# First condition by halves of the channels, weights and condition in separate slots: one change to a fused two-block kernel on one core

## What is computed

```python
c_act = silu(c)
cond = c_act @ ada_w + ada_b                     # 1024 x 6144 weights, one row
shift1, scale1, gate1, shift2, scale2, gate2 = split(cond, 6)
h = rmsnorm(x, norm1_g) * (1 + scale1) + shift1
u, v, val, gate = split(h @ w_in + b_in, 4)      # 512 columns each
y_a = rmsnorm(gelu(u) * mixed(layernorm(gelu(v))))
y_b = rmsnorm(silu(layernorm(conv31(val * sigmoid(gate)))))
x = x + gate1 * (concat(y_a, y_b) @ w_out)
# then a feed-forward with shift2, scale2, gate2 of 2816 columns, a final norm with its own condition
# then the second block: projections, sparse attention, cross attention, and 32 experts of three 1 MB matrices each
```

## Time and profile before

| what | value |
|---|---|
| three runs | 792.23, 792.97, 793.47 us; median 792.97 us |
| the profiled execution | 789.66 us, of it 787.9 us span of the core |
| PE busy | 719.9 us (91%), 5423 matmuls |
| DVE busy | 366.7 us (47%) |
| ACT busy | 326.4 us (41%) |
| bytes loaded | 209.5 MB, 267 GB/s over the span |

### The profile page before, as it was taken

One profiled execution on the slowest core, in us unless ns is written; L12 is line 12 of the kernel. 1 busy time (PEld: TensorE's weight loads), 2 busy tenths in 40 slices (PEclk: granted clock), 3 DMA queues, 4 the chain that ended last, 5 costly groups with the idle time before them and its releaser, 6 DMA issues.

```text
span 787.9 us, 13085 instructions
## 1 busy us (share of the span) xinstructions
PE 719.9 (91%) x5423; PEld 563.0 (71%) x5424; DVE 366.7 (47%) x745; ACT 326.4 (41%) x696; POOL 60.8 (8%) x71
## 2 busy tenths in 40 slices
PE   6798999889999999999999999997999998778785
PEld 4385678787999999999988777785865554344352
DVE  1452998554755444555478679544441111011011
ACT  2243485363743333454448896668421111001001
POOL 5000002000000000100000009062000000000000
PEclk9899899889999999999999999999999999899899
DMA  8997856633966656553554436355999999999994
GB/s 317 406 372 286 304 219 268 237 107 109 370 215 215 214 179 215 202 182 135 178 187 148 157 108 222 107 214 213 343 393 422 419 422 420 422 420 421 418 406 142
DMA packets 71476, 211.44 MB, mean 268 GB/s; under 512 B 7352, under 2 KB 34134, under 8 KB 55543
## 3 DMA queue, kind: packets, MB, share of 16 engines
q1 hardware_dynamic: 70370, 209.91, 70.3%
q0 software_dynamic: 800, 0.63, 0.5%
q10 hardware_dynamic: 244, 0.03, 0.0%
HBM read 209.51 MB, written 1.05 MB: 267 GB/s over the span
## 4 chain that ended last, share of the span: by engine, by line
PE 67%; DMA 15%; DVE 7%; ACT 6%; issue 3%; SPq 2%; ACTq 0%; DVEq 0%
PE ps L1906 10%; PE ps L1907 9%; PE ps L1908 9%; DMA ring<-in_expert_w_gate_dram 7%; PE ps L1919 5%; PE ps L2590 5%; PE ps L1920 5%; PE ps L1921 5%; DMA ring<-in_expert_w_up_dram 4%; PE ps L1988 3%; DMA ring<-in_ada_w_dram 2%; SPq L431 2%; DVE ring_low L1177 2%; PE ps L2632 2%; PE ps L2561 2%
## 5 line engine op out<-in xcount | busy, mean ns | idle before, releaser
L1177 DVE TENSOR_TENSOR ring_low<-ring,HI 128x1024 fp32r<-128x1024 f32 (+1 forms) x119 | 142.3, 1237 | 45.9 <-ACT HI L667 45.8
L667 ACT ACTIVATE HI<-ring 128x1024 fp32r<-128x1024 f32 (+1 forms) x135 | 133.9, 1056 | 42.4 <-DMA ring<-in_w_in_dram 41.4
L1906 PE MATMUL ps<-AH,HI 128*128 128x256 f32 x320 | 90.1, 282 | 0.3 <-DVE Z L1423 0.3
L1908 PE MATMUL ps<-AH,ring_low 128*128 128x256 f32 x320 | 89.6, 280 | 0.0
L1907 PE MATMUL ps<-AL,HI 128*128 128x256 f32 x320 | 89.5, 280 | 0.0
L2590 PE MATMUL ps<-ring,ZM 128*32 128x256 f32 x880 | 73.6, 422 | 16.1 <-DMA ring<-in_expert_w_up_dram 11.2
L1906 PE MATMUL ps<-HI,AH 128*128 128x512 f32 (+1 forms) x176 | 71.6, 407 | 2.1 <-DVE ring_low L1177 1.0
L1907 PE MATMUL ps<-ring_low,AH 128*128 128x512 f32 (+1 forms) x176 | 68.9, 392 | 0.0
L1908 PE MATMUL ps<-HI,AL 128*128 128x512 f32 (+1 forms) x176 | 68.5, 389 | 0.0
L2590 PEld LDWEIGHTS ps<-ring,ZM 128*32 128x32 f32 x880 | 35.1, 121 | 44.0 <-DMA ring<-in_expert_w_up_dram 14.1
L1906 PEld LDWEIGHTS ps<-AH,HI 128*128 128x128 f32 x320 | 60.1, 188 | 3.1 <-issue 2.5
(11 more groups left out here) (381 smaller groups left out, 1325.8 us busy)
## 6 DMA issues: line engine op xcount, KB each, us to landing
ring<-in_expert_w_up_dram SPq DMA_DIRECT2D x28, 1024.0 KB, 26.3
ring<-in_expert_w_gate_dram SPq DMA_DIRECT2D x27, 1024.0 KB, 26.4
ring<-in_ada_w_dram SPq DMA_DIRECT2D x24, 1024.0 KB, 8.6
ring<-in_expert_w_down_dram SPq DMA_DIRECT2D x23, 1024.0 KB, 23.8
ring<-in_w_ffn_in_dram SPq DMA_DIRECT2D x20, 1024.0 KB, 6.1
ring<-in_w_in_dram SPq DMA_DIRECT2D x17, 1024.0 KB, 5.7
ring<-in_w_ffn_out_dram SPq DMA_DIRECT2D x11, 1024.0 KB, 7.1
ring<-in_w_out_dram SPq DMA_DIRECT2D x8, 1024.0 KB, 4.9
```

The costliest lines, as they stand in the source:

```text
L667: act(HI[:, i % UNITS, 0:w], W.view(name)[:, o:o + w], ACT.Copy).then_inc(s_hi, 1)
L1177: tt(W.low(name)[:, o:o + w], W.view(name)[:, o:o + w], HI[:, i % UNITS, 0:w].bitcast(F32), ALU.subtract).then_inc(s_lo, 1)
L1906: mm(dst, lh, rh, start=start, stop=False)
L1908: return mm(dst, ll, rh, start=False, stop=stop)
```

## The change

1. `ada0k` is loaded and multiplied by halves of the channels. A load of 1 MB now holds 256 rows (two per partition) and, of both shift1 and scale1, the 512 columns of one half; it is issued as two transfers of 0.5 MB. PE does `ada_half(h, kp)`, eight matmuls of 32 by 256; four of them complete shift1 and scale1 for half of the channels, and `columns_half`, `lower_half(h)` on DVE and `upper_half(h)` on ACT make AH and AL for four channel tiles at a time.
2. Value and gate are multiplied by halves of the channels too: value units 0 and 1, gate units 0 and 1, then the second halves. The `ada1k` steps that stood between their units move into `between_v`, two after each unit; the `ada2k` steps move into `between_u` (0, 2, 3 and 3 of them). `condition(2, 7)` on DVE goes behind the normalisation of v, and PE's `columns(2, 7)` behind the first unit of u.
3. The eight slots are divided: four for `ada` loads, four for all others, until `out0`; then one ring again. The order of the loads is a new one.
4. v's bias is loaded to a row of `CN` instead of a slot.
5. The sums of squares of x come from two ACT instructions over whole rows (`accum_out`) instead of four squares by channel and PE's 16 products.
6. POOL waits for the first four `ada` steps before it issues its 17 small loads.

```diff
     def place(self, name, until, dmas=1):
-        s = self.order[self.turn % len(self.order)]
-        self.turn += 1
+        if self.lots is None:
+            s = self.order[self.turn % len(self.order)]
+            self.turn += 1
+        else:
+            lot = self.lots[not name.startswith(self.start)]
+            s = lot[0]
+            lot.append(lot.pop(0))
...
+            def ada_half(h, ks):
+                for k in ks:
+                    load(f"ada0{4 * h + k}", (s_ada, 4 * h + k + 1), *(
+                        (lambda v, i=i: v[:, 1024 * i:1024 * i + 1024].rearrange("p (s n) -> p s n", s=2),
+                         A["ada_w"][:, 0:2048].rearrange("(p k) (s n) -> p k s n", p=P, s=2)[:, 2 * k + i, :, 512 * h:512 * h + 512])
+                        for i in range(2)))
...
-            ada(A["ada_w"], 0, range(7), 0)
-            rows128("in_v0", w_in, 1024, 512, 0, 2)
-            ada(A["ada_w"], 0, (7,), 0)
-            rows128("in_v1", w_in, 1024, 512, 2, 4)
-            rows128("in_v2", w_in, 1024, 512, 6, 2)
-            ada(A["ada_w"], 1, (0, 1), 2048)
+            W.apart("ada", 4)
+            ada_half(0, range(4))
+            rows128("in_v0", w_in, 1024, 512, 0, 4)
+            ada_half(1, (0, 1))
+            rows128("in_g0", w_in, 1536, 512, 0, 4)
+            ada_half(1, (2, 3))
             const(wsv, ...)
-            rows128("in_g0", w_in, 1536, 512, 0, 4)
-            ada(A["ada_w"], 1, (2, 3), 2048)
-            rows128("in_g1", w_in, 1536, 512, 4, 4)
-            ada(A["ada_w"], 1, (4, 5), 2048)
-            load("brow_v", (s_un, S.first["in_u0"] + 1), (lambda s: s[0:1, 0:512], A["b_in"][:, 512:1024]))
+            rows128("in_v1", w_in, 1024, 512, 4, 4)
+            rows128("in_g1", w_in, 1536, 512, 4, 4)
+            sp.dma_start(brow_v, A["b_in"][:, 512:1024]).then_inc(*W.other(BROW))
             rows128("in_u0", w_in, 512, 512, 0, 4)
-            ada(A["ada_w"], 1, (6, 7), 2048)
+            ada(A["ada_w"], 1, (0, 1), 2048)
             rows128("in_u1", w_in, 512, 512, 4, 4)
-            ada(A["ada_w"], 2, (0, 1), 4096)
             sp.wait_ge(s_rp, 3)
             (the memory tokens, 1 MB)
+            ada(A["ada_w"], 1, (2, 3), 2048)
             rows128("in_w0", w_in, 0, 512, 0, 4)
-            ada(A["ada_w"], 2, (2, 3), 4096)
+            ada(A["ada_w"], 1, (4,), 2048)
             rows128("in_w1", w_in, 0, 512, 4, 4)
-            ada(A["ada_w"], 2, (4, 5), 4096)
+            ada(A["ada_w"], 1, (5, 6, 7), 2048)
             rows128("kv_v0", w_kv, 512, 512, 0, 4)
-            ada(A["ada_w"], 2, (6, 7), 4096)
+            ada(A["ada_w"], 2, (0, 1, 2, 3), 4096)
             rows128("kv_v1", w_kv, 512, 512, 4, 4)
-            for h in range(4):
+            ada(A["ada_w"], 2, (4, 5), 4096)
+            rows128("out0", w_out, 0, D, 0, 2)
+            ada(A["ada_w"], 2, (6, 7), 4096)
+            W.together([7, 0, 1, 2, 3, 4, 5, 6])
+            for h in range(1, 4):
...
+            po.wait_ge(s_ada, 4)
             const(rowsc[0:4 * TAPS, :], ...)            # POOL, the first of 17
...
+            for t in range(NT):                         # ACT
+                act(SQA[:, t, :], X[:, t, :], ACT.Square, accum_out=RTS[0][:, t:t + 1]).then_inc(s_sqs, 1)
+            def upper_half(h):
+                hi_to((0, 5)[h])
+                ac.wait_ge(s_m, h + 1)
+                for k in range(4 * h, 4 * h + 4):
+                    act(AH[:, k, :], XR[:, k, :], ACT.Identity, scale=..., bias=...).then_inc(s_ah, 1)
+                    if k % 4 == 1:
+                        hi_to(4 * h + 1)
+            upper_half(0)
+            hi_to(3)
+            upper_half(1)
+            hi_to(7)
...
+            def lower_half(h):                          # DVE
+                ve.wait_ge(s_ada, 4 * h + 4)
+                copy(CN[:, 0, 0:256], ps[7][:, 0:256]).then_inc(s_cn, 1)
+                if h:
+                    lo_to(4)
+                (columns and scales of four channel tiles)
+                for k0 in (4 * h, 4 * h + 2):
+                    (HTM of tiles k0, k0 + 1)
+                    if k0 == 0:
+                        lo_to(0)
+                    (AL of tiles k0, k0 + 1)
+                lo_to(4 * h + 1)
+            lower_half(0)
+            lo_to(3)
+            lower_half(1)
+            lo_to(7)
...
+            ve.wait_ge(s_un, S.first["in_u0"] + 1)      # DVE, ahead of E (line 1286)
...
             (DVE: v normalised, line 1312)
+            condition(2, 7)
+            taps(18, 20)
+            columns(2, 7, C2[:, B1:B1 + 16])
             lo_to(iw + 1 + AHEAD)
-            taps(18, 22)
+            taps(20, 22)
...
+            by_channel(("in_v0",), value, "value", (0, 1, 2, 3), between_first)    # PE; ada_half(1, 0), (1, 1) after unit 1
+            by_channel(("in_g0",), gate, "gate", (), between_second)               # ada_half(1, 2), (1, 3) after unit 0
+            columns_half(1)
...
+            by_channel(("in_v1",), value, "value", (), lambda q: None, 2)
+            by_channel(("in_g1",), gate, "gate", (), lambda q: None, 2)
...
             def between_v(i):
-                ada(2, i)
+                for k in ((0, 1), (2, 3), (4, 5), (6, 7))[i]:
+                    ada(1, k)
...
             def between_u(i):
-                ada(2, 4 + i)
+                if i == 0:
+                    columns(2, 7)
+                if i == 1:
+                    te.wait_ge(s_col, 3)
+                for k in ((), (0, 1), (2, 3, 4), (5, 6, 7))[i]:
+                    ada(2, k)
                 diagonals(3 + i)
```

More of the change, by code:

```diff
@@ L103, in split_order @@
 def split_order():
-    out = ["in_v0", "in_v1", "in_v2"] + [f"{w}{h}" for w in ("in_g", "in_u", "in_w", "kv_v") for h in "01"]
+    out = [f"{w}{h}" for h in "01" for w in ("in_v", "in_g")] + [f"{w}{h}" for w in ("in_u", "in_w", "kv_v") for h in "01"]
     out += [f"out{h}" for h in range(4)] + ["fx0", "fy0"]
@@ L735, in _ @@
                     ACT.Copy).then_inc(s_wt, 1)
-            for u in range(4, 8):
-                hi_to(u + AHEAD)
+            hi_to(S.first["in_u0"] + 1)
             ac.wait_ge(s_rc, 1)
@@ L1254, in _ @@
             copy(cw[:, :, 0:TAPS], ps[6][:, 0:4 * TAPS].rearrange("p (j c) -> p c j", c=4)).then_inc(s_rc, 1)
-            for u in range(4, 8):
-                lo_to(u + AHEAD)
-            condition(2, 7)
+            lo_to(S.first["in_u0"] + 1)
             ve.wait_ge(s_set, PAD)
@@ L1990, in ada, with ada_half, columns_half @@
                 ins.then_inc(s_ada, 1)
+            def ada_half(h, kp):
+                name = f"ada0{4 * h + kp}"
+                te.wait_ge(*W.ready(name))
+                for i in range(2):
+                    for j in range(4):
+                        ins = mm(ps[7][32 * j:32 * j + 32, 0:256], cr[:, 2 * kp + i, :],
+                                 W.view(name)[:, 1024 * i + 256 * j:1024 * i + 256 * j + 256],
+                                 start=(kp == 0 and i == 0), stop=(kp == 3 and i == 1))
+                ins.then_inc(s_ada, 1)
+            def columns_half(h):
+                te.wait_ge(s_cn, h + 1)
+                for x in range(2):
+                    ins = tr(ps[7][:, P * x:P * x + P], CN[:, 0, P * x:P * x + P], ident[:, :])
+                ins.then_inc(s_cnp, 1)
             def columns(i, b):
-                te.wait_ge(s_cn, i)
+                te.wait_ge(s_cn, i + 1)
                 for x in range(4):
@@ L2052, in by_channel, with value, gate, between_first @@
                     between(q)
+            def value(ct):
+                return ps[ct][:, 0:256]
+            def gate(ct):
+                return ps[ct][:, 256:512]
             te.wait_ge(s_xc, 4)
-            by_channel(("in_v0", "in_v1", "in_v2"), lambda ct: ps[ct][:, 0:256], "value", (0, 1, 2, 3), lambda q: q and ada(1, q - 1))
+            def between_first(q):
+                if q == 1:
+                    te.wait_ge(s_col, 1)
+                    ada_half(1, 0)
+                    ada_half(1, 1)
+            def between_second(q):
+                if q == 0:
+                    ada_half(1, 2)
+                    ada_half(1, 3)
+            by_channel(("in_v0",), value, "value", (0, 1, 2, 3), between_first)
+            by_channel(("in_g0",), gate, "gate", (), between_second)
+            columns_half(1)
             te.wait_ge(s_r2, 16 * LOADS2)
```

146 lines of the change are left out of this document (69 added, 77 removed).

## The result

The changed kernel takes 771.67 us (median of 3 runs, 769.43 to 774.03) against 792.97: ratio 0.9721, 95% interval 0.9687 to 0.9756, 21.3 us less. Forecast were 781.6 and a range of 774 to 790. The direction was right, and the size was short by 9.9 us. The profiled execution took 774.03 us (span 772.2), against 789.66 before. Here is the timeline of PE after the change, at the places that answer to the earlier trace rows.

A forecast was written before the change was run, and what follows sets the result against it. Before 140 us it took loads, PE, slot waits, then PE and DVE together as bounds in turn. Transposes 15.4 us earlier, less 4 for a clock fall, gave 11.4: 792.97 - 11.4 = 781.6 us, range 774 to 790.

The forecast's parts named there:

- The sum: Added-up times of the first stages: first value matmul 23.9, gate's end 56.4, v's start 57.4 us.
- the 1.34: PE's time for one `ada_half` step of 16 instructions, from the experts' matmuls at 0.084 us each: 1.34 us.
- the bound of 1.0: One `ada_half` step on PE takes 1.0 us if the columns set the pace, 2.0 if weight loads do.
- XR at 26: Before the first value matmul: with the old sums of squares XR, done at 26 us, would be 3 us late.
- the 6.99 us: PE's 16 products for the sums of squares: 6.99 us, most of it taken as waiting between squares.
- rival (b): First eight `ada` loads arrive late as halves, 5.6 us in all at 320 GB/s: 788.5 us, chance 0.18.
- the 2.93 us a load: First loads land 2.93 us apart per 1 MB, against 2.55 by the windows at 412 GB/s.
- I take a fall, and 4 us lost: Behind PE's 2.9 us wait at `columns(2, 7)`: clock falls, 4 us lost, memory's transposes 11.4 earlier, not 15.4.
- it shifts as a whole: What follows the first stages, PE nearly full from 200 us, moves unchanged with the end of those stages.
- the 1.97 us at 140.18: PE's wait behind the memory's transposes, taken to just cover 2.0 us of added `ada` steps in `between_u(3)`.
- the low end of 774: Better than the other cases: 2.55 us a load and `ada_half` at 1.0 give 774 us, chance 0.05.
- Rival (a): No fall of the clock at `columns(2, 7)`, or a shorter wait: 777.6 us, chance 0.25.

The follow-up runs named there:

- after_again: The changed kernel run again with nothing changed: 773.14 us, ratio 0.9777 to the kernel before; its profiled execution took 769.74 us.
- whole_condition: The changed kernel with the first `ada` weights loaded and used in whole steps, in the new load order: 786.8 us, ratio 0.9909 to the kernel before.
- old_squares: The changed kernel with the old sums of squares, by channel with products on PE: 778.63 us, ratio 0.9827 to the kernel before.
- before_filled: The kernel before with six useless matmuls ahead of `columns(2, 7)` and four in the wait at 140 us: 793.88 us, ratio 1.0023.
- longer_wait: The changed kernel with DVE's `condition(2, 7)` moved behind `taps(18, 20)`, lengthening PE's wait: 781.2 us, ratio 0.9852 to the kernel before.
- slots_3_5: The changed kernel with three slots for `ada` loads and five for the others: 788.62 us, ratio 0.9936 to the kernel before.
- the two delays: The changed kernel with two or four useless matmuls ahead of the feed-forward: 777.74 and 780.63 us, ratios 0.9861 and 0.9886 to the kernel before.
- the second series: Both kernels run again with nothing changed: kernel before 794.32 us, ratio 1.0015; changed kernel 773.14 us, ratio 0.9777.
- spatial_behind: The changed kernel with the spatial weights loaded behind in_g1 and transposed behind in_v1's units: 776.58 us, ratio 0.9782 to the kernel before.

## Why the prediction was right in part, and wrong in size

**Up to v, right but for a fall of the clock.** Forecast were the first value matmul at 23.9 (its own terms add up to 24.2), gate's end at 56.4 and v at 57.4. Measured were 22.73, 56.40 and 57.42 in `after_again`, and 23.21, 59.16 and 60.18 in the first profile, with a fall of the clock that I had put at nothing. The sum has about 2 us of pause there (42.7 to 44.8) and no term for the clock; in five of seven profiles it fell. in_v1 was there at 41.15 against 40.1. `ada_half` cost 1.07 us for its 16 instructions, not the 1.34 I took from the earlier trace rows: 16 instructions of 256 columns take what 8 of 512 take (1.07 and 1.06 us in `whole_condition`), so the columns streamed decide here, the bound of 1.0 that I had named. The sums of squares and POOL's loads cost nothing at gate's end, as said. But that XR at 26 would be late by 3 us was wrong, as `old_squares` shows (first value matmul at 25.04, 1.8 to 2.3 later, and none of it left at gate's end). So was the reading that most of the 6.99 us of the earlier trace rows is waiting between squares. The same 32 instructions take 3.94 us in `old_squares`, and 6.96 in `before_filled`, where the granted clock from 14 to 22 us is 0.50: for the most part it is the half rate. The record of the clock before reads 1.00 there, but the `ada` steps on either side take 1.94 and 1.93 us, their length at half rate.

The loads landed about as reckoned: in_v0 at 19.94 (forecast 21.1), in_g0 at 29.73 (29.8), in_v1 at 41.15 (40.1). But rival (b) did happen, in part. `whole_condition` has the same loads in the same order, as single transfers of 1 MB in pieces of 8 KB, and moves more. The windows are those of the first profile after, and then those of `whole_condition`:

```profile
8.00:12.00 4.00, 4.00 (x35) 2.91 (x37) 2.63 (x6) 2.33 (x5) 0.00 (x0) 1.00 1.05 389
12.00:16.00 4.00, 1.98 (x32) 0.68 (x24) 2.36 (x5) 0.00 (x0) 0.00 (x0) 1.00 1.05 387
```

```profile
8.00:12.00 4.00, 4.00 (x30) 2.29 (x28) 2.75 (x5) 1.92 (x5) 0.00 (x0) 1.00 1.02 429
12.00:16.00 4.00, 1.67 (x20) 0.21 (x16) 2.00 (x5) 0.00 (x0) 0.00 (x0) 1.00 0.98 404
```

Its in_v0 is there at 18.64, and its last `ada` load at 34.03, which in `after_again` PE waits for until 36.51. So the halves pay about 2.5 us of loading for what they gain, where the rival had 5.6 at 320 GB/s; the 2.93 us a load in the sum was long enough to cover it. The Trainium skill (DMA: Bandwidth & Descriptors, Rules for kernel authors) asks for at least 1 MiB a transfer for the most bandwidth. These windows agree in direction, but no run here separates the size of the transfer from its pieces of 2 KB.

**From v to the memory's transposes.** 51.5 us were forecast without a fall, and 50.78 measured in both profiles (60.18 to 110.96). The wait at `columns(2, 7)` was forecast at 2.9 us and measured at 2.41 and 0.86. The step that failed is "I take a fall, and 4 us lost". There was no fall behind that wait. The transposes came 16.0 us earlier without a fall that reached them and 13.2 with the one at 45, where I had 11.4. That a fall there was possible was right, as `longer_wait` shows with 4.86 us; its price was 2.8 us there and not 4. The inference from 3.17 and 3.07 in the kernel before to 2.9 was too sure. At this place five profiles with waits of 2.41 to 2.49 and four with 0.82 to 0.94 had no fall behind them; the ones of 2.66 (in `slots_3_5`) and 4.86 had one. So at this place only longer waits than the measured one fell, each in a single profile, and the one of 2.66 in a kernel whose `ada` loads came late. That the length decides is not shown: ahead of value's second half one length did both. The Trainium skill (TensorE: Matmul & The Clock Gate, What's actually happening) states that the chip watches activity by a schedule of its own, which isn't tied to the kernel. The pair of 2.94 and 2.95 there agrees with it. A forecast should have carried a chance for a fall at each of the two waits, instead of a fall taken into the sum at one and nothing at the other.

**Behind it.** The second failed step is that "it shifts as a whole". I had seen the 1.97 us at 140.18 only as cover for the two added `ada` steps, and reckoned nothing for the slow matmuls behind it. In the kernel before it takes 29.65 us from the first to the second squares, in both profiles. After, it takes 28.03 and 26.48: 1.6 to 3.2 us more gained. Behind the wait of 1.97 the clock fell, and the 16 matmuls of one column took 2.85 and 2.87 us, for what took 1.92 after; behind the 0.25 the 16 run at the full rate, as they do in `before_filled` with its wait filled (1.84). The 1.6 us between the two profiles after go with a brief fall from 128 to 134 us in the first. From the second squares to the end the distance is indeed the same: 618.1 and 617.1 before, 617.2 and 617.0 after. That all four of these profiles have it short is luck: eleven of the other thirteen have 619.4 to 627.6, the added matmuls of the two delays included.

**The sum again.** The two profiled executions on which the forecast is to be judged, 789.66 and 774.03, are 15.6 us apart: 13.2 at the transposes, 1.6 behind the first squares and 0.9 behind the second. The forecast had 11.4 between them, so 4.2 of the missing 9.9 us lie here, though a fall at 45 took 2.8 away. Against `after_again` (spans 787.9 and 786.7 to 767.7) it is 19.0 to 20.2 us: 11.4 as forecast, 4.6 more at the transposes (16.0 less 11.4) and 3.2 behind the first squares, 19.2.

The other 5.7 us are the step from profile to median. I had carried the 3.3 us by which the median of before lay above its profiled execution over to the changed kernel, whose median lies 2.4 below its own profile. It is not only the scatter of three executions: beside the later runs the medians of before were 793.2 to 794.2, and 773.1 for the changed kernel, some 20 us apart, and both profiles of before (789.66, 788.43) lie 3.5 to 6 us below these medians. What the slower executions of before lose that its two profiles don't show was not profiled, and stays open.

The nearest of the cases was the low end of 774, with a chance of 0.05, and for another reason: it let only the loads and `ada_half` be better, and neither the wait at 140 nor the spread of single executions. Rival (a), without the fall, had the right reason and 777.6.

**What the parts are worth.** The halves: 6.5 to 9.2 us at the transposes, 13.7 between the medians of the second series; between profiles 6.7 or 11.0, by which profile of the changed kernel is taken. Four slots for `ada` instead of fewer: needed, since three lose 9.75 us from gate to the transposes. The sums of squares and POOL's late start: nothing at gate's end. One undivided ring with the new order of loads, the moved `ada` steps and the bias row outside the ring were not tried alone.

## What to carry to other kernels

When a kernel waits for a set of weights before its first real work, ask whether half of the output needs only half of them: the pass over the other half then hides its loads and keeps buffers moving, even where the halved loads come in smaller pieces and a little slower. Price a wait on PE by what follows it at the half clock, as a chance and not as a certainty, and look for the places where the change removes such a wait as hard as for those where it adds one. Give the range room for the scatter of single executions, and don't forecast a median from one profile's offset.

## What the runs showed of the hardware

The granted clock can fall without any wait of PE of 1 us or more. It did so at 32 matmuls of one column each (4.81 us instead of 3.63, then 0.50 for at least 4 us), and in `after_again` at 60 us (0.57). Such a fall costs nothing where PE waits for another engine soon behind it: there it only shortened the next wait, from 2.41 to 0.86 us. Behind the second squares, a wait of 1.56 us and 16 matmuls of one column, the granted clock fell to 0.50 in all 17 profiles. Filling the two waits of the kernel before, so that the clock held there, made its second squares 3.1 us earlier counted from gate's end, and its end no earlier, in 12 executions (1.0023 [1.0003, 1.0043]).

Float32 loads in two transfers of 0.5 MB with pieces of 2 KB moved 387 to 389 GB/s with the queue full, single ones of 1 MB with pieces of 8 KB 404 to 429.

A matmul of 128x512 in plain float32 took 0.89 us (4.46 us for five, which the profile shows as ten instructions). The five were meant to fill 2.94 us.

Two issues of SP, in_v1 and in_g1 behind the spatial weights with their small pieces, took 9.18 us, as SP's own timeline after shows. In `spatial_behind`, where these pieces are issued later, the two took 5.55 us, and in `whole_condition` 12.62. The load itself was still there about when its bytes' turn came:

```profile
25.16 9.18 SPq L451 DMA_DIRECT2D ring<-in_w_in_dram  x2
```
